# A hybrid decoder step: state-space gating in groups of four tiles with one root, feed-forward norm scale behind the products, and early loads for the output projection

## The reference, cut to what matters

```python
yg = y.reshape(b, L, D_INNER) * jax.nn.silu(z.astype(jnp.float32))
yg = yg.reshape(b, L, SSD_GROUPS, D_INNER // SSD_GROUPS)
yg = yg * lax.rsqrt(jnp.mean(yg * yg, axis=-1, keepdims=True) + EPS)
yg = yg.reshape(b, L, D_INNER) * gnorm_w.astype(jnp.float32)
return (yg.astype(h.dtype) @ w_out).astype(h.dtype), new_ssm, new_conv
...
gu = h @ w_gu
return (jax.nn.silu(gu[..., :d_ff]) * gu[..., d_ff:]) @ w_down
```

## Time and profile before

| what | value |
|---|---|
| median of 3 runs (lowest, highest) | 1831.22 us (1830.47, 1832.38) |
| profiled execution | 1833.29 us |
| its span in the trace | 1831.5 us |
| PE busy | 1669.0 us, 91% of the span |
| DVE busy | 1360.4 us, 74% |
| ACT busy | 1071.4 us, 58% |
| chain that ended last: PE / DVE / ACT / issue / DMA | 72% / 11% / 7% / 7% / 2% |

### The profile page before, as it was taken

The page is one execution under the profiler, slowest core; times in us unless marked ns, Lnnn a source line. Parts: engine busy times, 40 slices in busy tenths (PEclk is TensorE's granted clock), DMA queues, the critical chain, the costliest instruction groups (busy, mean ns, idle before and its releaser), DMA issues.

```text
span 1831.5 us, 24965 instructions
## 1 busy us (share of the span) xinstructions
PE 1669.0 (91%) x9200; PEld 1418.5 (77%) x9200; DVE 1360.4 (74%) x1364; ACT 1071.4 (58%) x1070; POOL 51.7 (3%) x90
## 2 busy tenths in 40 slices
PE   3889993889998989969999999999999999999994
PEld 2787772889997989857878878778788788787783
DVE  1866996555545656568888888788798888888886
ACT  1753344344433544337777777777777776777774
POOL 1000110000000000000000000000000000000000
PEclk9988997999999989979999999999999999999997
DMA  7432763496456444439999999999999999999994
GB/s 102 145 109 67 249 232 107 127 247 181 140 154 211 141 136 141 161 126 358 358 362 366 347 374 357 358 368 357 359 369 358 363 360 352 373 358 347 376 362 131
DMA packets 303945, 480.22 MB, mean 262 GB/s; under 512 B 10814, under 2 KB 151342, under 8 KB 303830
## 3 DMA queue, kind: packets, MB, share of 16 engines
q1 hardware_dynamic: 290736, 446.95, 71.0%
q0 software_dynamic: 7712, 27.62, 5.6%
q10 hardware_dynamic: 5432, 4.78, 0.9%
HBM read 461.19 MB, written 18.32 MB: 262 GB/s over the span
## 4 chain that ended last, share of the span: by engine, by line
PE 72%; DVE 11%; ACT 7%; issue 7%; DMA 2%; ACTq 0%; DVEq 0%; POOLq 0%; POOL 0%
PE bank L1177 9%; PE bank L1179 9%; PE bank L1178 9%; PE bank L809 7%; PE bank L810 7%; PE bank L811 7%; PE bank L1198 5%; PE bank L1200 4%; PE bank L1199 4%; ACT part L747 2%; DVE part L1709 2%; PE bank L1163 1%; DMA raw_w<-in_sgu_b_in_dram 1%; DVE part L331 1%; ACT part L324 1%
## 5 line engine op out<-in xcount | busy, mean ns | idle before, releaser
L1709 DVE TENSOR_TENSOR part<-raw_w,part 128x2048 fp32r<-128x2048 f32 x336 | 763.3, 2292 | 141.0 <-ACT part L747 119.7
L747 ACT ACTIVATE part<-raw_w 128x2048 fp32r<-128x2048 f32 x336 | 642.9, 1918 | 258.0 <-PE bank L1179 167.8
L1177 PE MATMUL bank<-part,xh 128*128 128x512 f32 x896 | 359.0, 401 | 10.7 <-DVE part L1709 9.2
L1179 PE MATMUL bank<-part,xl 128*128 128x512 f32 x896 | 354.8, 396 | 0.0
L1178 PE MATMUL bank<-part,xh 128*128 128x512 f32 x896 | 354.7, 396 | 0.0
L331 DVE TENSOR_TENSOR part<-raw_w,part 128x2048 fp32r<-128x2048 f32 (+1 forms) x84 | 181.7, 2166 | 138.2 <-ACT part L324 138.0
L809 PE MATMUL bank<-ah,part 128*128 128x264 f32 x800 | 238.4, 298 | 10.5 <-DVE al L1242 7.2
L810 PE MATMUL bank<-ah,part 128*128 128x264 f32 x800 | 232.2, 290 | 0.0
L811 PE MATMUL bank<-al,part 128*128 128x264 f32 x800 | 232.1, 290 | 0.0
L1177 PEld LDWEIGHTS bank<-part,xh 128*128 128x128 f32 x896 | 168.8, 188 | 53.5 <-DVE part L1709 12.2
L1179 PEld LDWEIGHTS bank<-part,xl 128*128 128x128 f32 x896 | 168.6, 188 | 40.6
(11 more groups left out here) (331 smaller groups left out, 1955.6 us busy)
## 6 DMA issues: line engine op xcount, KB each, us to landing
raw_w<-in_moe_w_gu_dram SPq DMA_DIRECT2D x226, 1024.0 KB, 7.2
raw_w<-in_moe_w_down_dram SPq DMA_DIRECT2D x112, 1024.0 KB, 7.2
raw_w<-in_ffn_w_gu_dram SPq DMA_DIRECT2D x44, 512.0 KB, 5.3
raw_w<-in_ssd_w_in_dram SPq DMA_DIRECT2D x20, 1024.0 KB, 5.6
raw_w<-in_sgu_w_in_dram SPq DMA_DIRECT2D x16, 1024.0 KB, 5.3
raw_w<-in_ffn_w_down_dram SPq DMA_DIRECT2D x16, 704.0 KB, 4.5
raw_w<-in_state_ssm_dram POOLq DMA_DIRECT2D x16, 512.0 KB, 5.4
out_dram<-raw_w POOLq DMA_DIRECT2D x16, 512.0 KB, 4.8
```

Of the source, the lines that this page charges most:

```text
L747: act.activation(part[:, n % PARTS, 0, :], raw_w[:, q, :], ACT.Copy).then_inc(S("part1"), 1)
L1177: mm(out, x[0], w[0][:, k, :], start=(half == 0 and k == 0), stop=False)
L1179: ins = mm(out, x[1], w[0][:, k, :], start=False, stop=(half == 1 and k == 3))
L1709: tt(part[:, n % PARTS, 1, :], raw_w[:, q, :], part[:, n % PARTS, 0, :].bitcast(F32), ALU.subtract).then_inc(S("part2"), 1)
```

## The change

- **Gating in groups.** DVE multiplies four tiles at a time (128x1056), ACT squares four at a time, and PE sums all four groups into one bank of four rows: `gsel` is a 128x4 stationary with a column of ones for its group. One mean, one root, one reciprocal on 4x264; four matmuls spread the four rows over 128 partitions (`gr_mm`); DVE scales tile by tile from that bank, ACT copies and DVE subtracts four tiles at a time. A one-column root ahead (`spare`) loads the table.
- **Weight tiles 20 to 22** are loaded in the state loop, straight into the low half of `part` (`landing` is the same memory); ACT splits them in rounds 9, 11, 13, DVE in rounds 10 and 12 and behind the loop.
- **Convolution tail rows** are transposed and copied out in rounds 1, 2, 3, 5, 6, 7 (`KEPT`), the copies on ACT instead of DVE, with two small stores on POOL each.
- **Norm scale behind the products.** For the feed-forward, `ah`/`al` are split from the residual times the norm weights alone, as each tile of it is finished; the reciprocal root per token multiplies both products of each pair on DVE. Silu moves from the product to that result. `hf` has three buffers.

```diff
...
+        part = at("part", [P, PARTS, 2, SLOT], PART_AT, F32R)
+        landing = at("landing", [P, PARTS, 2, SLOT], PART_AT)
...
+        EARLY = (20, 21, 22)
...
+            if n in EARLY:
+                act.wait_ge(S("early_in"), 48)
+                act.activation(part[:, n % PARTS, 0, :], landing[:, n % PARTS, 1, :], ACT.Copy).then_inc(S("part1"), 1)
+                return
...
+        KEPT = [1, 2, 3, 5, 6, 7]
+        HP = [4, 9, 14, 16]
...
+            def early(n):
+
+                sp.wait_ge(*read({20: 11, 21: 9, 22: 10}[n]))
+                sp.dma_start(landing[:, n % PARTS, 1, :].rearrange("p (k n) -> p k n", k=IT), dense[n][0]).then_inc(S("early_in"), 16)
...
+                if 14 <= n < 17:
+                    early((21, 22, 20)[n - 14])
...
+                if t in KEPT:
+                    q = KEPT.index(t)
+                    c = slice(512 * q, 512 * q + 512)
+                    pool.wait_ge(S("ncv_ready"), q + 1)
+                    pool.wait_ge(S("conv_out"), 16 + 32 * q)
+                    pool.dma_start(o[3][0, 0, :, c], ncv[0:3, q % 2, :]).then_inc(S("conv_out"), 16)
+                    pool.dma_start(o[5][0, :, 2, c], ncv[3:11, q % 2, :]).then_inc(S("conv_out"), 16)
...
+                    if n in LATE:
+                        act.activation(ah[:, m, :], xT[:, m, :], ACT.Copy, scale=V[:, NORM[n] + m:NORM[n] + m + 1]).then_inc(S("a1"), 1)
...
+                    if t in KEPT:
+                        q = KEPT.index(t)
+                        act.wait_ge(S("misc"), misc + 1)
+                        if q >= 2:
+                            act.wait_ge(S("conv_out"), 16 + 32 * (q - 1))
+                        act.activation(ncv[:, q % 2, :], psum[5 + misc % 2][0:11, :], ACT.Copy).then_inc(S("misc_free"), 1)
+                        misc += 1
+                        act.wait_ge(S("misc_free"), misc)
+                        act.nop().then_inc(S("ncv_ready"), 1)
...
+                    if t in (9, 11, 13):
+                        split_1(act, 20 + (t - 9) // 2)
...
-            for n in range(20, 23):
-                split_1(act, n)
             for g in range(G):
-                for k in range(4):
-                    n = 4 * g + k
-                    act.wait_ge(S("gated"), n + 1)
-                    act.wait_ge(S("sq_used"), DT + n - 1)
-                    act.activation(sq[:, n % 2, :], zT[:, n, :], ACT.Square).then_inc(S("sq_ready"), 1)
-
-                for g_ in ([g - 1] if g else []) + ([g] if g == G - 1 else []):
-                    act.wait_ge(S("gms_ready"), g_ + 1)
-                    act.activation(rs[:, 1, :], rs[:, 0, :], ACT.Sqrt).then_inc(S("groot_ready"), 1)
-                    for n in range(4 * g_, 4 * g_ + 4):
-                        act.wait_ge(S("yg_ready"), n + 1)
-                        act.activation(zh[:, n, :], zT[:, n, :], ACT.Copy).then_inc(S("yg1"), 1)
-            norm(1, IT, lambda m: split_1(act, 22 + m) if m else None)
+                act.wait_ge(S("gated"), g + 1)
+                if g >= 2:
+                    act.wait_ge(S("sq_used"), DT + g - 1)
+                act.activation(sqg[:, g % 2], zT[:, 4 * g:4 * g + 4, :], ACT.Square).then_inc(S("sq_ready"), 1)
+            act.activation(spare, ones[:, 0:1], ACT.Sqrt).then_inc(S("groot_ready"), 1)
+            act.wait_ge(S("gms_ready"), 1)
+            act.activation(rs[0:G, 1, :], rs[0:G, 0, :], ACT.Sqrt).then_inc(S("groot_ready"), 1)
+            for g in range(G):
+                act.wait_ge(S("yg_ready"), 4 * g + 4)
+                act.activation(zh[:, 4 * g:4 * g + 4, :], zT[:, 4 * g:4 * g + 4, :], ACT.Copy).then_inc(S("yg1"), 1)
+            norm(1, G, lambda m: split_1(act, 22 + m) if m else None)
...
             for n in range(FT + 1):
                 if n < FT:
                     split_1(act, SSD_TILES + n + 2)
-                    act.wait_ge(S("ffn"), n + 1)
-                    if n >= 2:
-                        act.wait_ge(S("ffn_h"), n - 1)
-                    act.activation(fs[:, n % 2, :], psum[2 * (n % 2)][:, 0:T], ACT.Silu).then_inc(S("ffn_silu"), 1)
+                    act.wait_ge(S("ffn_rs"), 2 * n + 1)
+                    act.activation(fs[:, n % 2, :], fs[:, n % 2, :], ACT.Silu).then_inc(S("ffn_silu"), 1)
...
-                    act.activation(hh[:, n - 1, :], hf[:, (n - 1) % 2, :], ACT.Copy).then_inc(S("ffn_h1"), 1)
+                    act.activation(hh[:, n - 1, :], hf[:, (n - 1) % 3, :], ACT.Copy).then_inc(S("ffn_h1"), 1)
...
+                if t in KEPT:
+                    q = KEPT.index(t)
+                    pe.wait_ge(S("misc_free"), misc - 1)
+                    for k in range(4):
+                        ins = tr(psum[5 + misc % 2][0:11, P * k:P * k + P], tail[:, 4 * q + k, :], ident[:, :])
+                    ins.then_inc(S("misc"), 1)
+                    misc += 1
...
             for g in range(G):
-                if g >= 2:
-                    pe.wait_ge(S("gms_ready"), g - 1)
+                pe.wait_ge(S("sq_ready"), DT + g + 1)
                 for k in range(4):
...
-
...
+                    ins = mm(psum[7][0:G, 0:T], gsel[:, g, :], sqg[:, g % 2, k, :], start=(g == 0 and k == 0),
+                             stop=(g == G - 1 and k == 3))
+                ins.then_inc(S("sq_used"), 1)
+            pe.wait_ge(S("z_ready"), IT)
+            pe.wait_ge(S("groot_ready"), 3)
+            for g in range(G):
+                mm(psum[1 + g][:, 0:T], ident[0:G, g:g + 1].to_broadcast((G, P)), rs[0:G, 0, :], start=True, stop=True
+                   ).then_inc(S("gr_mm"), 1)
...
-            out_proj(20, 1, (zh, zl), "yg2", 1, IT)
+            out_proj(20, 1, (zh, zl), "yg2", 1, G, 4)
...
                 if p >= 2:
-                    pe.wait_ge(S("ffn_h"), p - 1)
+                    pe.wait_ge(S("ffn_rs"), 2 * (p - 1))
...
-                for m in range(DT + 1):
...
+                if t in (10, 12):
+                    split_2(dve, 20 + (t - 10) // 2)
...
             y_out(IT - 1)
             dve.wait_ge(S("y_done"), IT)
-            for t in range(IT):
-                dve.wait_ge(S("gate_ready"), t // 4 + 1)
-                tt(zT[:, t, :], zT[:, t, :], xbc[:, t, :], ALU.mult).then_inc(S("gated"), 1)
...
+            split_2(dve, 22)
+            for g in range(G):
+                dve.wait_ge(S("gate_ready"), g + 1)
+                tt(zT[:, 4 * g:4 * g + 4, :], zT[:, 4 * g:4 * g + 4, :], xbc[:, 4 * g:4 * g + 4, :], ALU.mult).then_inc(S("gated"), 1)
+            dve.wait_ge(S("sq_used"), DT + G)
+            ts(rs[0:G, 0, :], psum[7][0:G, 0:T], G / DI, EPS, ALU.mult, ALU.add).then_inc(S("gms_ready"), 1)
+            dve.wait_ge(S("groot_ready"), 2)
+            dve.reciprocal(rs[0:G, 0, :], rs[0:G, 1, :]).then_inc(S("groot_ready"), 1)
+
+            def yg_low(g):
+
+                dve.wait_ge(S("yg1"), g + 1)
+                tt(zl[:, 4 * g:4 * g + 4, :], zT[:, 4 * g:4 * g + 4, :], zh[:, 4 * g:4 * g + 4, :].bitcast(F32),
+                   ALU.subtract).then_inc(S("yg2"), 1)
+
+            for g in range(G):
+                dve.wait_ge(S("gr_mm"), g + 1)
+                for n in range(4 * g, 4 * g + 4):
+                    stt(out=zT[:, n, :], in0=zT[:, n, :], scalar=V[:, GN + n:GN + n + 1], in1=psum[1 + g][:, 0:T],
+                        op0=ALU.mult, op1=ALU.mult).then_inc(S("yg_ready"), 1)
+                if g:
+                    yg_low(g - 1)
+            yg_low(G - 1)
             dve.nop().then_inc(S("ssd_over"), 1)
...
+                stt(out=al[:, m, :], in0=xT[:, m, :], scalar=V[:, NORM[n] + m:NORM[n] + m + 1], in1=ah[:, m, :].bitcast(F32),
+                    op0=ALU.mult, op1=ALU.subtract).then_inc(S("a2"), 1)
...
                     tt(xT[:, m, :], xT[:, m, :], psum[m % 2][:, 0:T], ALU.add).then_inc(S("x_ready"), 1)
+                    if m and n in LATE:
+                        a_low(n, m - 1)
+                if n in LATE:
+                    a_low(n, DT - 1)
...
-                    dve.wait_ge(S("ffn_silu"), n + 1)
...
+                    tt(fs[:, n % 2, :], psum[2 * (n % 2)][:, 0:T], rs[:, 0, :], ALU.mult).then_inc(S("ffn_rs"), 1)
+                    tt(hf[:, n % 3, :], psum[2 * (n % 2) + 1][:, 0:T], rs[:, 0, :], ALU.mult).then_inc(S("ffn_rs"), 1)
+                if 1 <= n <= FT:
+                    dve.wait_ge(S("ffn_silu"), n)
+                    dve.wait_ge(S("ffn_rs"), 2 * n)
+                    tt(hf[:, (n - 1) % 3, :], fs[:, (n - 1) % 2, :], hf[:, (n - 1) % 3, :], ALU.mult).then_inc(S("ffn_h"), 1)
+                if n >= 2:
+                    dve.wait_ge(S("ffn_h1"), n - 1)
+                    dve.wait_ge(S("ffn_h"), n - 1)
+                    tt(hl[:, n - 2, :], hf[:, (n - 2) % 3, :], hh[:, n - 2, :].bitcast(F32), ALU.subtract).then_inc(S("ffn_h2"), 1)
...
```

More of the change, by code:

```diff
@@ L76, in hybrid_step @@
         raw_w = sb("raw_w", [P, RAW, SLOT])
-        part = sb("part", [P, PARTS, 2, SLOT], F32R)
         xT = sb("xT", [P, DT, T])
@@ L168, in hybrid_step @@
         dd = r.take(4)
```

(37 more changed lines are left out.)

82 lines of the change are left out of this document (32 added, 50 removed).

## The result

The changed kernel takes 1790.12 us (median of four runs, 1789.17 to 1790.51) against 1830.98 us of the kernel before on the same chip: a ratio of 0.9775, with a 95% interval from 0.9758 to 0.9792. The forecast was 1804.4 us and its range ended at 1799.5: the gain is 40.9 us, not 26.8. The profiled executions took 1790.03 us (span 1788.0) and 1833.29 us (span 1831.5).

The account below looks back on a forecast made before the run. Bound: a chain of waits across engines behind the state loop, then PE from the feed-forward to the end. Terms 4.0 - 23.6 - 7.2 = -26.8 us, from the median 1831.22 to 1804.4; range 1799.5 to 1812.

Parts of the forecast that it names:

- The loop, +4.0: State loop: the weight splits and tail-row transposes moved into it cost 4.0 us, bounds 2.2 and 8.
- The tail rows: State loop: PE's transposes make its output 0.26 us late in rounds 4 and 8, 0.52 us in all.
- the second split's: State loop: DVE's weight split in round 12 fills its 0.93 us wait in round 13, so costs 1.27 us.
- The gating, -23.6: Last `y_out` to the output projection's first finished tile: 54.9 us become 31.3, bounds 28.1 and 38.
- The half-clock rival: Gating: PE stays at half clock all through, +6.3 us, 1810.7 us in all; chance 0.12.
- The feed-forward's start, -7.2: Feed-forward: its first product no longer waits for the root and ends at 383.05 instead of 390.29 us; low bound -4.3.
- The pairs, 0: Feed-forward: a pair still takes 5.80 us despite two more multiplications on DVE, with 0.14 us to spare.
- the ring: Feed-forward, rival: the ring through DVE and ACT binds, +6 us at 0.5 a pair, 1810.4 us; chance 0.05.

Follow-up runs that it names:

- e2: The changed kernel with `part` back at byte 82048, all other edits kept: 1804.98 us (ratio 0.9853).
- e5: The changed kernel with the feed-forward's norm as before (root ahead of the products, Silu straight from the product's bank): 1795.88 us (ratio 0.9799).

## Why the prediction was wrong

- **The step that failed** is in its first part: "From there to the end PE is the path, and whatever is gained ahead of it moves everything behind it". That PE is the path is right; that the stages behind it only move, at their old pace, is wrong: in the experts a matmul's step went from 0.233 to 0.227 us, and an item from 124.83 to 122.83. The prediction went through the change part by part and never priced the diff's line that moves `part`, which the split weights pass through; 14.9 us (e2 against the changed kernel) lay in it. The sum of what was priced, 1804.4, was met by e2 with 1804.98.
- **The loop, +4.0:** 4.65 at its end, 4.9 by its own length. The tail rows cost 0.5, as worked out. The mis-sized piece is the second split's: it did not fill the wait in round 13. DVE still waits 0.37 us for ACT there (264.54, in place of 0.93 in the earlier trace rows) and 0.37 again in the round behind (271.17), so the two splits cost 4.4 to 4.6, not 3.5.
- **The gating, -23.6:** -24.3. The sums began 4.65 us behind the last `y_out` (at 289.86), as worked out, and the reciprocal 14.7 behind it for 15.0. The granted clock over its course (window, its length, busy time of each engine, clock, DMA):

```profile
290.00:292.00 2.00, 2.00 (x5) 0.52 (x4) 2.00 (x2) 0.98 (x1) 0.00 (x0) 0.50 0.00 0
292.00:294.00 2.00, 2.00 (x7) 0.70 (x6) 0.20 (x1) 0.36 (x1) 0.00 (x0) 0.62 0.00 0
294.00:296.00 2.00, 2.00 (x11) 0.78 (x9) 0.00 (x0) 1.25 (x2) 0.00 (x0) 1.00 0.00 0
...
304.00:310.00 6.00, 2.85 (x13) 2.87 (x14) 6.00 (x12) 3.25 (x3) 0.00 (x0) 0.50 0.00 0
311.00:316.00 5.00, 4.30 (x36) 4.08 (x35) 2.97 (x4) 1.08 (x1) 0.00 (x0) 1.00 0.02 3
```

  The clock rises within the sums, falls once more while PE waits between the groups, and is full again for the last steps of the first tile. The Trainium skill ("TensorE: Matmul & The Clock Gate", section "HAM oscillation — how this bites in real kernels") has the clock throttled in such bursts; by the trace that is true of 304 to 310 us, where PE waits for DVE anyway, and it did not reach the end of the stretch. The half-clock rival falls.
- **The feed-forward's start, -7.2:** 7.05 in the trace of e5. **The pairs, 0:** 5.80 us before and after; the ring does not bind.
- **What else moved.** In the mixer of the second layer the lead grew to 30.1 us (its last addition at 738.64 instead of 768.71), and shrank to 27.9 ahead of the experts. Two windows of the kernel before, and then the two about the same places of the changed one (clock third from the right):

```profile
652.00:658.00 6.00, 5.56 (x25) 5.56 (x26) 0.39 (x2) 0.00 (x0) 0.00 (x0) 0.52 0.64 175
...
786.00:792.00 6.00, 5.99 (x42) 4.72 (x40) 4.70 (x18) 0.41 (x1) 0.54 (x1) 0.77 0.21 38
```

```profile
624.00:629.00 5.00, 3.09 (x25) 3.09 (x26) 1.85 (x4) 0.16 (x1) 0.00 (x0) 1.00 0.54 157
...
757.00:763.00 6.00, 6.00 (x30) 4.91 (x30) 3.67 (x14) 0.00 (x0) 0.53 (x1) 0.50 0.35 81
```

  The granted clock fell at other places. In the first windows the same 25 matmuls keep PE busy for 5.56 us before and for 3.09 now; in the second, the same 18 small matmuls (L1116, there L1162) last 1.93 us before (from 788.99) and 3.69 now (from 759.02). The lead moved by +3.3 and -2.2 us, so most of that is the clock's, and no term foresaw it.
